# Second attention: the scores of four heads in one stretch of the matmul engine

## The reference, cut to what matters

```python
z = hn @ w_in[l]
q_lat, kv_lat, k_rope, u_pool, gate_a, gate_b = jnp.split(z, IN_SPLITS, axis=-1)
...
# mla_attention, 8 heads of 64 + 32, query blocks of 128 that read only the keys up to their end
sc = (q_nope @ k_nope.T + q_rope @ k_rope.T) * scale
p = softmax(where(k_chunk <= q_chunk, sc, -inf)) ; outs.append(p @ v)
# multiscale_pool, four groups of 128 channels
y = einsum('bsgc,gce->bsge', trailing_mean(u) - u, group_w) * scale
...
h = h + (sigmoid(gate_a) * (attn @ w_attn_branch) + sigmoid(gate_b) * (pool @ w_pool_branch)) @ w_mix_out
```

## Time and profile before

| | |
|---|---|
| median of 3 runs | 947.66 us (947.3 to 948.8) |
| the profiled execution, its own time | 948.02 us |
| its span, first to last instruction | 946.2 us |
| TensorE busy | 933.3 us, 99% of the span |
| VectorE busy | 532.9 us, 56% |
| ScalarE busy | 469.6 us, 50% |
| DMA | 223.55 MB, mean 236 GB/s |

### The profile page before, as it was taken

How to read it: one execution, slowest core, us unless ns; L and a number is a source line. 1 busy time by engine, 2 the same in 40 slices (tenths; PEclk the granted TensorE clock), 3 DMA queues, 4 the chain that set the end, 5 groups by cost and what they waited for, 6 DMA issues and landing times.

```text
span 946.2 us, 14062 instructions
## 1 busy us (share of the span) xinstructions
PE 933.3 (99%) x5793; PEld 760.3 (80%) x5793; DVE 532.9 (56%) x835; ACT 469.6 (50%) x728; POOL 4.3 (0%) x13
## 2 busy tenths in 40 slices
PE   9999999999999999999999999999999999999996
PEld 8989887888889999999889888889876665666553
DVE  5888996775766555655686875676454212122213
ACT  5588846857354444444566756445452131313113
POOL 1000000000000000000000000000000000000000
PEclk9999999999999999999999999999999999999999
DMA  9945565535555555554645735476758999999993
GB/s 317 314 143 168 188 223 178 163 105 179 178 185 194 178 178 178 178 185 152 210 151 178 231 131 165 147 252 238 273 187 299 409 409 408 409 409 409 408 409 136
DMA packets 89862, 223.55 MB, mean 236 GB/s; under 512 B 9162, under 2 KB 14019, under 8 KB 89795
## 3 DMA queue, kind: packets, MB, share of 16 engines
q1 hardware_dynamic: 87488, 219.62, 65.2%
q10 hardware_dynamic: 2306, 2.99, 0.9%
HBM read 221.54 MB, written 1.05 MB: 235 GB/s over the span
## 4 chain that ended last, share of the span: by engine, by line
PE 95%; DMA 2%; DVE 1%; ACT 0%; issue 0%; POOL 0%; POOLq 0%
PE pb L494 22%; PE pb L496 21%; PE pb L495 21%; PE pb L2508 11%; PE pb L2531 5%; PE pb L2548 3%; DMA my<-in_w_exp_down 2%; PE pb L2482 2%; PE pb L584 2%; PE pb L664 1%; PE pb L652 1%; PE pb L751 1%; PE pb L635 1%; PE pb L728 1%; PE pb L602 1%; PE pb L558 1%
## 5 line engine op out<-in xcount | busy, mean ns | idle before, releaser
L1567 DVE TENSOR_TENSOR wl<-raw,wh 128x2048 fp32r<-128x2048 f32 (+3 forms) x112 | 246.3, 2208 | 96.5 <-ACT wh L1017 96.2
L1017 ACT ACTIVATE wh<-raw 128x2048 fp32r<-128x2048 f32 (+3 forms) x112 | 206.7, 1852 | 110.3 <-PE pb L496 102.0
L494 PE MATMUL pb<-wh,th 128*128 128x512 f32 (+2 forms) x620 | 245.8, 397 | 0.0
L496 PE MATMUL pb<-wh,tl 128*128 128x512 f32 (+2 forms) x620 | 238.9, 385 | 0.0
L495 PE MATMUL pb<-wl,th 128*128 128x512 f32 (+2 forms) x620 | 238.6, 385 | 0.0
L494 PE MATMUL pb<-th,wh 128*128 128x256 f32 x528 | 152.7, 289 | 0.0
L495 PE MATMUL pb<-tl,wh 128*128 128x256 f32 x528 | 149.3, 283 | 0.0
L496 PE MATMUL pb<-th,wl 128*128 128x256 f32 x528 | 149.3, 283 | 0.0
L496 PEld LDWEIGHTS pb<-wh,tl 128*128 128x128 f32 x620 | 116.4, 188 | 23.4
L494 PEld LDWEIGHTS pb<-wh,th 128*128 128x128 f32 x620 | 116.5, 188 | 22.9 <-issue 2.2
L495 PEld LDWEIGHTS pb<-wl,th 128*128 128x128 f32 x620 | 116.6, 188 | 20.7
(11 more groups left out here) (424 smaller groups left out, 1117.4 us busy)
## 6 DMA issues: line engine op xcount, KB each, us to landing
raw<-in_w_in SPq DMA_DIRECT2D x31, 1024.0 KB, 5.9
raw<-in_w_up SPq DMA_DIRECT2D x16, 1024.0 KB, 5.7
raw<-in_w_down SPq DMA_DIRECT2D x16, 1024.0 KB, 5.2
raw<-in_w_exp_gate SPq DMA_DIRECT2D x9, 1024.0 KB, 18.5
raw<-in_w_xkv SPq DMA_DIRECT2D x8, 1024.0 KB, 5.1
raw<-in_w_exp_down SPq DMA_DIRECT2D x8, 1024.0 KB, 18.0
raw<-in_w_exp_up SPq DMA_DIRECT2D x7, 1024.0 KB, 16.1
my<-in_w_exp_down SPq DMA_DIRECT2D x7, 1024.0 KB, 17.4
```

Source lines behind the costliest of these rows:

```text
L494: PE.matmul(o, lh, rh, start=start, stop=False, skip_group_check=True)
L496: return PE.matmul(o, ll, rh, start=False, stop=stop, skip_group_check=True)
L1017: ACTE.activation(hi_of(i), raw_of(i), ACT.Copy).then_inc(S["hi"], 1)
L1567: DVE.tensor_tensor(lo_of(i), raw_of(i), hi_of(i).bitcast(F), ALU.subtract).then_inc(S["lo"], 1)
```

## The change

The scores of a set are computed for all four heads in one stretch, each head in a bank of its own (0 to 3), by a new function `pe_scores_wide`. For set 4 it stands before slot 4 of unit (1, 0), where heads 0 and 1 stood. For set 5 it stands before slot 7 of unit (1, 1) and waits for the fourth `pool_lo`, since the pooling used banks 2 and 3. The pooling's products stay before slot 3 of unit (1, 1), and wait now for the four masks of set 4 as well. VectorE's masks are taken from banks 0 to 3 by a new function; their place in its order is the same. ScalarE's list is untouched.

```diff
+        def pe_scores_wide(n):
+
+            if n == 4:
+                PE.wait_ge(S["t2"], 8)
+            else:
+                PE.wait_ge(S["sc_add"], 4 * n)
+                PE.wait_ge(S["pool_lo"], 4)
+            for b, h in enumerate(heads_of(n)):
                 PE.matmul(PB[b][:, 0:128], att_lhs(n, h, 0), att_rhs(n, h, 0, 128), start=True, stop=True, skip_group_check=True)
                 PE.matmul(PB[b][:, 128:384], att_lhs(n, h, 1), att_rhs(n, h, 0, 256), start=False, stop=True,
                           skip_group_check=True).then_inc(S["sc_mm"], 1)
...
-        def pe_pool():
+        def pe_pool(scored):
             PE.wait_ge(S["d_poolw"], 16)
+            PE.wait_ge(S["sc_add"], scored)
             PE.wait_ge(S["pooled"], 8)
             PE.wait_ge(S["t2"], 8)
...
-                        (1, 0): {4: scores_4},
-                        (1, 1): {0: lambda: pe_scores(4, 1), 3: pe_pool, 5: lambda: pe_scores(5, 0)},
-                        (2, 0): {1: lambda: pe_scores(5, 1)},
+                        (1, 0): {4: lambda: pe_scores_wide(4)},
+                        (1, 1): {3: lambda: pe_pool(4 * 4 + 4), 7: lambda: pe_scores_wide(5)},
+                        (2, 0): (),
...
+        def dve_masked_wide(n):
+
+            SS = SSV[n].rearrange("p (h n) -> p h n", h=4)
+            if n == 4:
+                DVE.wait_ge(S["t2"], 8)
+            for i in range(4):
+                DVE.wait_ge(S["sc_mm"], 4 * n + i + 1)
+                DVE.tensor_tensor(SS[:, i], PB[i][:, 0:384], cst("mask2", 384), ALU.add).then_inc(S["sc_add"], 1)
...
-            dve_masked(4, 0)
-            dve_masked(4, 1)
+            dve_masked_wide(4)
...
-            dve_masked(5, 0)
-            dve_masked(5, 1)
+            dve_masked_wide(5)
```

More of the change, by code:

```diff
@@ L629, in pe_scores @@
                     PE.wait_ge(S["sc_add"], 4 * n + i - 1)
-                elif n not in (0, 4):
-                    if i == 0 and n not in (1, 5):
+                elif n > 0:
+                    if i == 0 and n > 1:
                         PE.wait_ge(S["pt"], 4 * (n - 2) + 4)
                     PE.wait_ge(S["sc_add"], 4 * (n - 1) + 3 + i)
+                PE.matmul(PB[b][:, 0:128], att_lhs(n, h, 0), att_rhs(n, h, 0, 128), start=True, stop=True, skip_group_check=True)
+                PE.matmul(PB[b][:, 128:384], att_lhs(n, h, 1), att_rhs(n, h, 0, 256), start=False, stop=True,
+                          skip_group_check=True).then_inc(S["sc_mm"], 1)
+        def pe_scores_wide(n):
[5 more added lines that the diff above has]
+            for b, h in enumerate(heads_of(n)):
                 PE.matmul(PB[b][:, 0:128], att_lhs(n, h, 0), att_rhs(n, h, 0, 128), start=True, stop=True, skip_group_check=True)
@@ L917, in pe_main @@
                 pe_tokens(("w_kv_up_2", b), 0, 1, 1, 4, 512, (lambda kk: (S["turn_lo"], TB_["k"] + kk - 3)) if b == 0 else None)
-            def scores_4():
-                PE.wait_ge(S["t2"], 8)
-                pe_scores(4, 0)
             at_gates = {(0, 0): {6: lambda: pe_turn2(0, lambda t, h: QM[:, t, 96 * h:96 * h + 96])},
                         (0, 1): {5: lambda: pe_turn2(1, lambda t, h: KC[:, t, h, :])},
-                        (1, 0): {4: scores_4},
-                        (1, 1): {0: lambda: pe_scores(4, 1), 3: pe_pool, 5: lambda: pe_scores(5, 0)},
-                        (2, 0): {1: lambda: pe_scores(5, 1)},
+                        (1, 0): {4: lambda: pe_scores_wide(4)},
+                        (1, 1): {3: lambda: pe_pool(4 * 4 + 4), 7: lambda: pe_scores_wide(5)},
+                        (2, 0): (),
                         (2, 1): {4: lambda: (PE.wait_ge(S["pool_lo"], 4), pe_turn_probs(4, 0, 24)),
@@ L1732, in dve_masked @@
                 DVE.wait_ge(S["pt_mm"], 4 * (n - 2) + 4)
-            if n == 4 and two == 0:
-                DVE.wait_ge(S["t2"], 8)
             for i in (2 * two, 2 * two + 1):
                 DVE.wait_ge(S["sc_mm"], 4 * n + i + 1)
-                DVE.tensor_tensor(SS[:, i], PB[i % 2][:, 0:384], cst("mask1" if n < 4 else "mask2", 384),
-                                  ALU.add).then_inc(S["sc_add"], 1)
+                DVE.tensor_tensor(SS[:, i], PB[i % 2][:, 0:384], cst("mask1", 384), ALU.add).then_inc(S["sc_add"], 1)
+        def dve_masked_wide(n):
[5 more added lines that the diff above has]
+                DVE.tensor_tensor(SS[:, i], PB[i][:, 0:384], cst("mask2", 384), ALU.add).then_inc(S["sc_add"], 1)
         def dve_max(n):
```

## The result

| | before | after |
|---|---|---|
| median, 20 runs each | 948.12 us | 950.83 us |
| range | 947.01 to 949.91 | 949.35 to 958.15 |
| ratio, with its 95% interval | | 1.0033, 1.0026 to 1.004 |

The change makes the kernel slower by 2.7 us by the medians, 3.1 us (2.5 to 3.8) by the ratio. The forecast was 950.4 us, from a median of before of 947.66 us in 3 runs and an added 2.74. The median of before over 20 runs is 0.46 us higher, so the added time is the fairer test: 2.74 against 2.7 and 3.1, within the interval.

A forecast was written before the change was run, and what follows sets the result against it. TensorE, busy 99% of the span, was taken as the bound. Pauses of 1.53 and 1.23 us less 0.02 us saved gave 2.74 us, added to 947.66 us: 950.4 us, range 949.9 to 951.0, chance 0.75.

The forecast's parts named there:

- Two heads cost 1.32 us: TensorE, gates stage: two heads' scores take 1.32 us, one head within a pair 0.66 us.
- a merged stretch saves next to nothing: TensorE: merging four stretches into two saves 0.02 us, bounds 0 to 0.40 us.
- 0.20 us per switch: Bound for TensorE: a switch between kinds of product, paid once per stretch, would save 0.40 us for two stretches.
- The wait for four masks: TensorE before the pooling: masks of set 4 end near 552.5, 2.6 us before 555.14, so it costs nothing.
- The low parts: VectorE: the fourth low part of the pooling comes 1.32 us later, at 561.07.
- the first pause: TensorE before set 5's scores, waiting for the fourth `pool_lo`: 1.53 us, bounds 0 to 1.6.
- The second pause: TensorE before set 4's transposes, waiting for probabilities ready 2.85 us later, at 573.81: 1.23 us, bounds 0 to 1.3.
- The delay reaches the end: Weight stream in the last 200 us: its refills move along with TensorE, so nothing of 2.74 us is counted back.
- B: Weight stream doesn't follow TensorE, so waits of 1.15 us near the end are used up: 949.3 us, chance 0.06.
- C: Between 571 and 716 us a TensorE wait for a transfer absorbs the delay: not slower, 947.6 us, chance 0.06.
- rival A: Only the pause before set 5's scores counts; the division is ready when TensorE comes: 949.2 us, chance 0.10.
- Rival D: TensorE's clock falls to the 1.2 GHz level in a pause, adding about 3 us: 953.4 us, chance 0.03.

The follow-up runs named there:

- e5: The changed kernel with only set 4 in one stretch, set 5 in two pairs as before; 0.1 us over before (-0.8 to 0.9).
- e7: The changed kernel with low parts ahead of the maxima and set 4's transposes two slots later; 0.3 us over before (-0.6 to 1.1).
- e9: The changed kernel with set 5's scores before slot 1 of (2, 0) and low parts ahead of the maxima; ratio 0.9997 to before.
- e2: The changed kernel with set 5's scores two slots later, before slot 1 of (2, 0); 0.0 us over before (-0.9 to 0.9).
- e6: The changed kernel with only set 5 in one stretch, set 4 in two pairs as before; 1.7 us over before (0.9 to 2.6).
- e3: The changed kernel with VectorE's low parts of the pooling ahead of the maxima of set 4; 1.1 us over before (0.3 to 2.0).
- e1: The changed kernel run and profiled again, nothing altered; 2.7 us over before (1.8 to 3.6).
- e8: The changed kernel with set 5's scores before slot 5 of (1, 1) instead of slot 7; 5.9 us over before (4.5 to 7.1).
- e11: Again the changed kernel with set 5's scores before slot 5 of (1, 1), on another chip; 5.5 us over before (4.2 to 6.8).
- e10: The changed kernel with set 5's scores before slot 3 of (1, 1); 7.8 us over before (6.4 to 9.1).
- e4: The changed kernel with the transposes of set 4 two slots later, value products and next transposes moved along; 2.0 us over before (1.0 to 2.9).

## Why the prediction was right

- *Two heads cost 1.32 us, a merged stretch saves next to nothing.* Right. With one stretch merged and no pause (`e5`) the stage is 0.06 us shorter, with two (`e7`, `e9`) 0.08 and 0.10, against the 0.02 forecast. The 0.20 us per switch that I kept as a bound would have shown as 0.4 in `e9`.
- *The wait for four masks is free.* Right: they end at 550.14 + 1.94 = 552.08, the pooling starts at 554.75.
- *The low parts come 1.32 us later, and make the first pause.* Right: they end at 560.69 + 0.33 = 561.02, forecast 561.07. The pause is 1.60 instead of 1.53: TensorE came at 559.24 + 0.33 = 559.57, 0.07 earlier than I had it, and the start behind the low parts took 0.15 instead of 0.10. The scores start at 561.17, as forecast.
- *The second pause comes from the end of unit (1, 1).* Right: the division ends at 573.89 in the clock of before, forecast 573.81; the pause is 1.26, forecast 1.23. The division is 0.08 later than forecast because the first head behind the first pause takes 0.73 us (560.84 to 561.57) and not 0.66. It takes 0.73 in each kernel here whose scores of set 5 had to wait, even for a quarter of a microsecond (`e2`, `e6`), and 0.66 in those without a wait; the reason isn't shown. I had left that out. The transposes so start 2.84 us late (573.66 + 0.33 against 571.15), forecast 2.76. What the merged stretch saves is not seen there, since the first pause only begins that much earlier.
- *The second pause doesn't depend on the length of the first.* This follows from the prediction's working, and the runs bear it out: the bracket before the transposes is 1.09 or 1.10 us with a first bracket of none (`e3`, `e6`), 1.44 (`e1`), 2.8 (`e8`, `e11`) and 4.20 us (`e10`). A first pause delays TensorE and the end of unit (1, 1) alike; only the two heads moved into the unit delay the one and not the other.
- *The delay reaches the end.* Right, 2.63 of 2.87 us, see `e1_again`. Rivals B and C fall with it, rival A with `e3` and `e4`, where each pause counts by itself.
- *Rival D, the clock.* Not in the changed kernel: 1.00 in the windows behind both pauses, as here from 561 to 565 us.

```profile
561.00:565.00 4.00, 4.00 (x23) 3.54 (x23) 2.90 (x6) 0.56 (x1) 0.00 (x0) 1.00 0.17 61
```

But its mechanism is real. By the profiled executions, a bracket of 1.44 us was followed by no fall of the clock, one of 2.8 us by a fall in one of two, and the one of 4.20 us by a fall. The price, which I had put at some 3 us, is 1.7 us in the one execution that can be set beside the same kernel without a fall, and by estimate 1.65 with the scores before slot 3.

What stays open is the cause of the clock of 0.95 in one run of the changed kernel; no other of its 30 runs had it.

## What to carry to other kernels

On an engine that is busy all the time, work moved ahead of the end of a unit is also a delay for everyone who waits for that end: count it once per such end, follow the copy, the split and the softmax behind it, and see how much margin their reader has (0.19 us here). A merged stretch gains nothing by itself when its parts cost the same apart; its place decides, and two slots later, or one swap on VectorE and a later reader, took the loss away (0.23 us of stage left in the one case, none in the other). Two halves of a change can cost more together than they do apart, when one makes a semaphore late and the other starts to wait for it.

## What the runs showed of the hardware that I had not expected

The same kernel with the same pause of 2.8 us had its clock fall in one profiled execution and not in the other, a difference of 1.7 us in the stage; so a dose of idle time has no single price in that region. And in the run with the clock of 0.95 the full 32-bit products took longer (the first 64 expert products 7.34 us as against 7.06), while the split products kept their 0.227 us from start to start (544.79 to 548.19 us, 15 products, 3.40 us).
